# Gated delta layer, sample tokens: four heads stacked on 128 rows instead of one head at a time

## The reference, cut to what matters

```python
gc = jnp.cumsum(gc, axis=-1)
a_mat = bc[..., :, None] * einsum('nbhid,nbhjd->nbhij', kc, kc) * decay_strict + eye(L)
rhs = concatenate([bc[..., None] * vc, (bc * exp(gc))[..., None] * kc], axis=-1)
sol = triangular_solve(a_mat, rhs, lower=True, unit_diagonal=True)
aqk = einsum('nbhid,nbhjd->nbhij', qc, kc) * decay_incl
def step(S, c):
    u = wv_c - einsum('bhlk,bhkv->bhlv', wk_c, S)
    o = einsum('bhlk,bhkv->bhlv', qg_c, S) + einsum('bhij,bhjv->bhiv', aqk_c, u)
    S = gl_c[..., None, None] * S + einsum('bhlk,bhlv->bhkv', kd_c, u)
    return S, o
```

## Time and profile before

| what | value |
|---|---|
| median of 3 runs | 3318.43 us |
| lowest, highest | 3312.52, 3320.44 us |
| the profiled execution | 3321.11 us, its span 3319.2 us |
| mean granted clock of PE over the span | 0.942 of 2.4 GHz |
| gated delta stage, output of the projection to the next stage | about 1811 to 2244 us of the span |
| data moved | HBM read 385.00 MB, written 14.57 MB |

### The profile page before, as it was taken

The page is one execution under the profiler, slowest core; times in us unless marked ns, Lnnn a source line. Parts: engine busy times, 40 slices in busy tenths (PEclk is TensorE's granted clock), DMA queues, the critical chain, the costliest instruction groups (busy, mean ns, idle before and its releaser), DMA issues.

```text
span 3319.2 us, 62869 instructions
## 1 busy us (share of the span) xinstructions
PE 3116.9 (94%) x28140; PEld 2778.6 (84%) x28140; DVE 1560.3 (47%) x2515; ACT 1076.9 (32%) x1630; POOL 146.8 (4%) x261
## 2 busy tenths in 40 slices
PE   7998998999999899999999998689999989998998
PEld 6995788799999665999998677359999957787997
DVE  4644543465564124464653534235556544534554
ACT  3432222344443122343432322013444332222342
POOL 1000001100000110000000100100000000011000
PEclk9999998899999896999998999569999999998999
DMA  7452401353635451445444230215454424111541
GB/s 221 146 164 80 141 4 32 102 169 130 195 129 200 154 193 52 135 145 186 155 130 153 102 106 8 63 51 175 131 188 146 145 72 153 52 29 44 164 138 67
DMA packets 333440, 402.41 MB, mean 121 GB/s; under 512 B 14746, under 2 KB 287295, under 8 KB 332813
## 3 DMA queue, kind: packets, MB, share of 16 engines
q1 hardware_dynamic: 320176, 353.20, 32.8%
q0 software_dynamic: 13072, 46.41, 4.8%
HBM read 385.00 MB, written 14.57 MB: 120 GB/s over the span
## 4 chain that ended last, share of the span: by engine, by line
PE 91%; DVE 5%; ACT 2%; issue 1%; POOL 0%; DMA 0%; DVEq 0%; ACTq 0%; POOLq 0%
PE bank L804 17%; PE bank L806 17%; PE bank L805 17%; PE bank L837 11%; PE bank L1417 4%; PE bank L1108 2%; PE bank L913 2%; PE bank L799 2%; PE bank L873 1%; PE bank L889 1%; PE bank L1652 1%; PE bank L1087 1%; PE bank L1639 1%; PE bank L1061 1%; PE bank L1192 1%
## 5 line engine op out<-in xcount | busy, mean ns | idle before, releaser
L804 PE MATMUL bank<-h_hi,w_hi 128*128 128x288 f32 x2816 | 837.0, 297 | 5.5 <-DVE h_lo L2119 5.5
L805 PE MATMUL bank<-h_hi,w_lo 128*128 128x288 f32 x2816 | 831.3, 295 | 0.0
L806 PE MATMUL bank<-h_lo,w_hi 128*128 128x288 f32 x2816 | 828.5, 294 | 0.0
L2127 DVE TENSOR_TENSOR w_lo<-ring,w_hi 128x2048 fp32r<-128x2048 f32 (+1 forms) x304 | 611.1, 2011 | 413.6 <-ACT w_hi L1736 413.6
L1736 ACT CAST w_hi<-ring 128x2048 fp32r<-128x2048 f32 (+1 forms) x304 | 511.1, 1683 | 613.1 <-PE bank L806 568.6
L804 PEld LDWEIGHTS bank<-h_hi,w_hi 128*128 128x128 f32 x2816 | 528.2, 188 | 6.7 <-DVE w_lo L2127 6.0
L806 PEld LDWEIGHTS bank<-h_lo,w_hi 128*128 128x128 f32 x2816 | 530.8, 188 | 0.0
L805 PEld LDWEIGHTS bank<-h_hi,w_lo 128*128 128x128 f32 x2816 | 529.1, 188 | 0.6
L804 PE MATMUL bank<-hid_hi,w_hi 128*128 128x288 f32 x1408 | 416.1, 296 | 0.0
L805 PE MATMUL bank<-hid_hi,w_lo 128*128 128x288 f32 x1408 | 415.4, 295 | 0.0
L806 PE MATMUL bank<-hid_lo,w_hi 128*128 128x288 f32 x1408 | 414.3, 294 | 0.0
(11 more groups left out here) (516 smaller groups left out, 3550.5 us busy)
## 6 DMA issues: line engine op xcount, KB each, us to landing
ring<-in_ffn_w_gate SPq DMA_DIRECT2D x88, 1024.0 KB, 5.5
ring<-in_ffn_w_up SPq DMA_DIRECT2D x88, 1024.0 KB, 8.0
ring<-in_ffn_w_down SPq DMA_DIRECT2D x64, 768.0 KB, 4.7
ring<-in_ffn_w_down SPq DMA_DIRECT2D x64, 640.0 KB, 5.9
ring<-in_rwkv_w_rkv SPq DMA_DIRECT2D x24, 1024.0 KB, 7.3
ring<-in_gdn_w_in SPq DMA_DIRECT2D x16, 1024.0 KB, 7.2
ring<-in_attn_w_qkv SPq DMA_DIRECT2D x12, 1024.0 KB, 6.4
ring<-in_rwkv_w_o SPq DMA_DIRECT2D x8, 1024.0 KB, 6.5
```

Source lines behind the costliest of these rows:

```text
L804: nc.tensor.matmul(out, w_hi_k, x_hi_k, start=start, stop=False)
L805: nc.tensor.matmul(out, w_lo_k, x_hi_k, start=False, stop=False)
L806: return nc.tensor.matmul(out, w_hi_k, x_lo_k, start=False, stop=stop)
L2127: nc.vector.tensor_tensor(w_lo[e][:, 0:k, :], raw, w_hi[e][:, 0:k, :], ALU.subtract).then_inc(w_lo_ready, 1)
```

## The change

The sample tokens of four heads are stacked on 128 partitions: head 4a + q has its 32 tokens on partitions 32q to 32q + 31 (ROWS), so there are two stacks (a = 0, 1) instead of eight heads of 32 partitions. The gates of the samples are projected into that layout, with four columns a product instead of 16.

Token-major copies, Gram matrices and decays of all eight heads come right after the start of the first ladder, and their two-level inverse between its levels. All eight states of a stack are held at a time (S0[0], S0[1], 2 MB each): the first four heads are loaded where the first two were, the other four after chunk 2's read, into memory of the first ladder. State reads stand between the pieces of chunks 2 and 3. The reads of four heads share one bank, are copied once, turned once, and solved with a product for each head. Decays of the sample states go from DVE to POOL; keys masked by sequence are made by POOL (sKmask) instead of masked u by DVE. The updates are four rounds, each of two halves (four sequences) of one stack: 16 products of 32 x 128 weights with 128 columns that take turns over the four row groups and write four banks, and four DVE additions of 128 x 512. Rounds 0 and 1 stand before the head norms, round 2 inside them, round 3 inside the projection. The norms and the projection use banks 4 to 7 first, and PE waits for the fifth addition to x before the next stage. POOL's mask and decay products come after the convolution instead of in it. Stores of the first four heads are issued after round 1, of the others after round 3.

```diff
-                for k in range(CH):
-                    last = nc.tensor.matmul(bank[4][0:NS, 64:80], h[:, k, SEQ:], w[:, k, :], start=(k == 0), stop=(k == CH - 1))
+                    for q, r in enumerate(ROWS):
+                        last = nc.tensor.matmul(bank[4][r, 64:68], h[:, k, SEQ:], w[:, k, :].rearrange(...)[:, q], ...)
...
+                gdn_read(2)
+                gdn_turn(1)
+                sample_read(0)
+                gdn_solve(2)
+                sample_read(1)
+                gdn_query(2)
+                gdn_update(2)
+                sample_read(2)
+                sample_read(3)
+                gdn_read(3)
+                gdn_turn(2)
+                sample_turn_read(0)
+                gdn_solve(3)
+                gdn_query(3)
+                sample_read(4)
+                gdn_update(3)
+                for hd in (5, 6, 7):
+                    sample_read(hd)
                 gdn_turn(3)
+                sample_turn_read(1)
+                for a in range(2):
+                    gdn_sample_solve(a)
                 after(goT_ready)
+                for a in range(2):
+                    gdn_sample_output(a)
+                after(seq_rows_ready, 2)
                 after(gs_ready)
+                sample_update(0)
+                after(got_ready, 2)
+                for a in range(2):
+                    last = nc.tensor.transpose(bank[3][:, 128 * a:128 * a + 128], sO[:, a, :], ident)
+                last.then_inc(goT_raw, 1)
+                after(goT_ready)
+                sample_update(1)
+                pe.wait_ge(gs_ready, NCHUNK + 1)
+                head_norms(0, 4, GDN_NORM_BANK, lambda: sample_update(2))
+                after(og_ready, 4)
...            (round 3 before block 2 of the projection; before block 4 a wait for its additions)
+                square(b + 9, W(GO_), 4, last_updates)
+                pe.wait_ge(x_updated, 8 * (s + 1) + 5)
...
+            def sample_matrices_gdn():
+                for i, src in enumerate((2, 1)):
+                    for a in range(2):
+                        for q, r in enumerate(ROWS):
+                            last = nc.tensor.matmul(bank[4 + i][r, 128 * a:128 * a + 128], W(src)[:, q + 4 * a, SEQ:], ident, ...)
+                for a in range(2):
+                    for q, r in enumerate(ROWS):
+                        last = nc.tensor.matmul(bank[6][r, 64 * a:64 * a + 64], W(1)[:, q + 4 * a, SEQ:], work[:, 0:2, q + 4 * a, SEQ:], ...)
+                after(g_spread)
+                for a in range(2):
+                    for r in ROWS:
+                        last = nc.tensor.matmul(bank[7][r, 32 * a:32 * a + 32], sG[r, a, :], const("causal4")[r, 0:32], ...)
+            def sample_inverse_start():      # 16 products, after level 2; sample_inverse_y and _x: 8 each, level 3
+            def sample_read(hd):
+                a, q = divmod(hd, 4)
+                if q == 0:
+                    after(gstate_in[a], 64)
+                for b_ in range(DEC_B):
+                    c0 = SEQ + DEC_T * b_
+                    last = nc.tensor.matmul(out[:, :, q, b_, :], S0[a][:, q, b_, :], work[:, 0:2, hd, c0:c0 + DEC_T], ...)
+            def gdn_sample_solve(a):
+                after(sr_ready)
+                for r in ROWS:
+                    last = nc.tensor.matmul(bank[a][r, 0:128], sXT[r, a, :], sR[r, a, :], start=True, stop=True)
+            def sample_update(i):            # PE
+                a, bh = divmod(i, 2)
+                if i >= 2:
+                    pe.wait_ge(gs_ready, NCHUNK + i)
+                for j in range(4):
+                    for q, r in enumerate(ROWS):
+                        last = nc.tensor.matmul(bank[ROUND_BANK[i][q]][:, 128 * j:128 * j + 128], sKmask[r, 4 * bh + j, a, :], sU[r, a, :], ...)
...
+                def sample_update(i):        # DVE
+                    after(gs_raw)
+                    after(gs_decayed)
+                    for q in range(4):
+                        part_ = S0[a][:, q, 4 * bh:4 * bh + 4, :].rearrange("p b n -> p (b n)")
+                        last = TT(part_, part_, bank[ROUND_BANK[i][q]][:, :], ALU.add)
...
+                def decayed_states(a):       # POOL
+                    for bh in range(2):
+                        part_ = S0[a][:, :, 4 * bh:4 * bh + 4, :]
+                        nc.gpsimd.tensor_tensor(part_, part_, egLs[...].broadcast_to([128, 4, 4, 128]), ALU.mult)
...
+                for a in range(2):           # POOL
+                    pool.wait_ge(gs_ready, NCHUNK + 2 + 2 * a)
+                    for q in range(4):
+                        pool.dma_start(dst[4 * a + q], S0[a][:, q]).then_inc(gstate_stored[a], 16)
```

More of the change, by code:

```diff
@@ L657, in program @@
+        sQK, sN, sY, sXT = (hflat[:, 2048 + 64 * i:2112 + 64 * i].rearrange("p (a n) -> p a n", n=32) for i in range(4))
+        sRead = cut(8192, (2, 2, 128))
+        sO = cut(8704, (2, 128))
+        sKmask = work[:, 2, :, 0:256].rearrange("p b (a n) -> p b a n", a=2)
+        ROUND_BANK = ((4, 5, 6, 7), (0, 1, 2, 3), (0, 1, 2, 3), (0, 1, 2, 3))
+        GDN_NORM_BANK = (5, 6, 7, 4, 5, 6, 7, 4)
         conv_in = shift_in
@@ new lines, in sample_inverse_start @@
+            def sample_inverse_start():
+                after(gtok_ready)
+                after(inv_start)
+                for a in range(2):
+                    for w in range(2):
+                        for r in ROWS:
+                            xt, one = sY[r, a, :], const("ident32")[r]
+                            last = nc.tensor.matmul(bank[4][r, 64 * a + 32 * w:64 * a + 32 * w + 32], one if w else xt, xt if w else one,
+                                                    start=(a == 0 and w == 0), stop=False, skip_group_check=True)
+                last.then_inc(inv_raw, 1)
@@ new lines, in sample_inverse_y, with sample_inverse_x @@
+            def sample_inverse_y():
+                after(inv_ready)
+                for a in range(2):
+                    for r in ROWS:
+                        last = nc.tensor.matmul(bank[5][r, 32 * a:32 * a + 32], sN[r, a, :], sX[r, a, 0, :], start=True, stop=True)
+                last.then_inc(invy_raw, 1)
+            def sample_inverse_x():
+                after(invy_ready)
+                for a in range(2):
+                    for r in ROWS:
+                        last = nc.tensor.matmul(bank[4][r, 64 * a + 32:64 * a + 64], sY[r, a, :], sX[r, a, 1, :],
+                                                start=False, stop=True, skip_group_check=True)
+                last.then_inc(inv_raw, 1)
@@ L1555, in gdn_inverse @@
                     gdn_query(0)
+                else:
+                    sample_matrices_gdn()
                 for l in range(1, LADDER):
@@ L1573, in gdn_inverse @@
                             gdn_turn(0)
+                    else:
+                        if l == 3:
+                            sample_inverse_y()
+                        if l == 4:
+                            after(inv_ready)
                     for g in range(2):
@@ L1583, in gdn_inverse @@
                         last.then_inc(inv_raw, 1)
+                    if not p and l == 2:
+                        sample_inverse_start()
+                    if not p and l == 3:
+                        sample_inverse_x()
                 if p:
@@ L2648, in gdn @@
-                dve.wait_ge(goT_ready, 4 + GH)
+                read(2)
+                solve(2)
+                update(2)
+                read(3)
+                solve(3)
+                sample_rhs(0)
+                update(3)
+                sample_rhs(1)
+                for a in range(2):
+                    after(su_raw)
+                    V.tensor_scalar(sU[:, a, :], bank[a][:, 0:128], gcol[:, BETA, 2, a:a + 1], None, ALU.mult).then_inc(su_ready, 1)
+                for a in range(2):
+                    last = V.tensor_scalar(sO[:, a, :], bank[2 + a][:, 0:128], gcol[:, EGC, 2, a:a + 1], None, ALU.mult)
@@ L2649, in gdn @@
+                link(last)
+                for a in range(2):
+                    after(go2_raw)
+                    TT(sO[:, a, :], sO[:, a, :], bank[a][:, 128:256], ALU.add).then_inc(got_ready, 1)
+                for i in range(2):
+                    sample_update(i)
+                dve.wait_ge(goT_ready, NCHUNK + 1)
                 for c in range(CH):
```

454 lines of the change are left out of this document (177 added, 277 removed).

## The result

The changed kernel took 3213.56 us (median of four runs, 3207.45 to 3219.08), the one before 3317.75 (3312.52 to 3320.44): a ratio of 0.9687, 95% interval 0.9664 to 0.9711. The forecast was 3217, range 3202 to 3240. The profiled execution took 3219.08 us, span 3216.4, against 3321.11 and 3319.2, so 102 us less where the working had 101.

The account below looks back on a forecast made before the run. Bound: a serial chain per head, ending on PE each time. B to F sum to 100.5 us against 205.4; with A, -101 from 3321.1 gives 3220, and 3217 as the runs' median (range 3202 to 3240).

Parts of the forecast that it names:

- the likeliest case: Whole kernel: the stage's chain shortened, the clock falling in some reads and recovering; 3217 us, chance 0.46.
- A: Sample work moved into the earlier prompt ladder, where PE is the bound, adds +4 us (3 to 7).
- B: Chunk 2's read to the sample solve: two chunk turns and eight state reads take about 39 us.
- C: Sample solve and first update round, until head sums may start: 7.5 us (5.7 to 10).
- D: Head norms, with round 2 in the reciprocal's wait: 16 us (12.1 to 18.1).
- E: Output projection plus round 3 on PE: 35.4 us (32.2 to 37.5).
- F: Stage's end: late state stores hold up weight casts and additions to x, +2.6 us (1 to 8).
- Rival 1: The clock stays at 2.4 GHz through the stage: a gain of 122.5 us, 3196 us; chance 0.14.
- rival 2: The clock is low from the first read to the projection: a gain of 84 us, 3234 us; chance 0.20.
- Rival 3: Groups don't overlap in the inserted products and update rounds: +16 us, 3233 us; chance 0.09.
- Rival 4: The second four states' stores land 13 us later, during the projection: 3230 us; chance 0.08.

Follow-up runs that it names:

- e6: Kernel after with all eight sample state reads in one block behind chunk 3's update: 3220.43 us, ratio 0.9715.
- e8: Kernel after with only one of the eight products of each state read: 3188.61 us.
- e2: Kernel after with each row group's four update products issued one after another instead of in turn: 3214.97 us.
- e3_double: Kernel after with the samples' token-major and Gram products issued twice in the ladder: 3205.92 us.
- e10: Kernel before with the next head's read issued behind the output product, its copy later, and a third state buffer: 3291.6 us, ratio 0.9923.
- e13_decays_late: Kernel after with GpSimd's decay of the first four states waiting for the last chunk: 3208.35 us, ratio 0.968.
- e11_wide_fill: Kernel after with wider reads, three unused products in the reciprocal's wait, and the reciprocal behind five of eight DVE products: 3200.38 us, ratio 0.9652.
- e4_no_store: Kernel after with the stores of the second four sample states left out: 3209.34 us.
- e1_wide: Kernel after with each state read product taking its own and all later sequences' columns, 64 down to 8: 3211.35 us, ratio 0.9686.
- e5_fill: Kernel after with five unused 288-column products in PE's wait for the norms' reciprocal: 3206.57 us, ratio 0.9676.
- e12_after_again: Kernel after, unchanged, run again as the measure for the others: 3213.9 us, ratio 0.9684.

## Why the prediction was right, point by point

The mechanism was that of the likeliest case: one chain in place of eight, PE without idle time through reads and projection, the clock in between. The sizes, forecast against the two profiles of the kernel after (first, again):

| term | forecast | first | again |
|---|---|---|---|
| A, into the ladder | +4 | +0.9 | +2.5 |
| B, reads and chunks | 39 | 37.3 | 33.1 |
| C, solve and round | 7.5 | 5.8 | 6.8 |
| D, norms | 16 | 14.5 | 16.3 |
| E, projection | 35.4 | 35.3 | 34.9 |
| F, late at the end | +2.6 | +1.2 | +1.1 |
| rest of the program | 0 | +7.2 | +8.1 |

*A* was too large. The 128 inserted records are there at the size forecast (3.4 us, each group counted to the start of the next product; 3.3 forecast), but the four column groups of the gate projection took no time on top of what was there (64 records in 1.04 us, as 16 did before), and the ladder has one low stretch of 3.4 us fewer in the first profile. With two of them in both kernels the difference is 2.5.

*B* was right in its mean (clock 0.70 and 0.80 around a forecast of 0.75): full clock first, a fall in the first reads, recovery, a fall in the last. But the clock fell four times in the first profile and not twice. Two readings of the working were off as well: its rows add up to 5.97 us of PE a chunk and not 5.7, and the earlier trace rows leave 3.4 us of idle for both chunks together and not 2.3 for each. The forecast's reason for the order, that the reads fill the gaps of the chunks, counts for little: e6 has the chunks alone at 13.6 us with 1.8 idle. The reads are added time, and their price is doubled by the clock that they bring down (e8). Rival 1 (no fall) and rival 2 (a fall throughout) are both refuted by the windows; e8 shows rival 1's clock when the reads are taken out, e6 most of rival 2's when they are not interrupted.

*C*: the terms that the working names (2.15 for the small steps, 1.7, 2.8) add up to 6.65, and it takes 7.5 without saying why. A round takes 1.17 us, not 1.7, and the four additions 2.5, not 2.8. The Trainium skill (TensorE: Matmul & The Clock Gate, Part 3), from which the prediction worked out an estimate of about 35 ns a record beside its own term, was the nearer of the two. Rival 3 (the groups do not overlap) is the kernel e2: its rounds cost 4.0 us more each at the low clock, as that rival had it, but 1.7 more at the full one, and the stage 7.7 and not 16. What decides between the two is the order of the issue.

*D and E* were right within 1.5 us. *F* had the right chain and nearly its times: the stores landed 25.4 us into the projection (forecast 26), the first addition to x began at 32.0 (32.4). The additions then came every 0.80 us, not every 0.97, so the norm was held up 1.1 to 1.2 us and not 2.6. Rival 4 (stores 13 us late) did not occur.

What failed is a sentence that the prediction did not write: that the rest of the program keeps its time. Ladder and stage together came out 9.6 us better than forecast (174.4 against 164.8, the norm's start included) and the rest 7.2 us worse, so that the total met this closely is luck: two errors of opposite sign. Thirteen profiles of this study have the same instructions behind the stage, and their time there goes with how long the clock is low in it:

| profile | clock low in the rest, us | rest, us |
|---|---|---|
| e3_double | 56.2 | 1064.5 |
| e10 (kernel before, early read) | 62.9 | 1067.8 |
| e13_decays_late | 65.5 | 1071.5 |
| before | 69.4 | 1071.8 |
| e8_few_reads | 72.6 | 1069.0 |
| e2_no_turns | 72.9 | 1072.0 |
| e11_wide_fill | 73.0 | 1073.3 |
| e6_reads_late | 79.8 | 1075.4 |
| e4_no_store | 85.5 | 1076.2 |
| e1_wide | 86.5 | 1076.0 |
| e5_fill | 86.6 | 1075.9 |
| after | 92.5 | 1079.0 |
| e12_after_again | 97.1 | 1079.9 |

From the first row to the last it is 15.4 us for 40.9, so 0.38 us for each microsecond of low clock. That the clock differs there though the code is the same is measured; that it depends on the moment at which the program arrives there fits, but no run set that moment by itself, and it stays open. The part ahead of the ladder speaks against the edits as the only cause: it begins with the program and no experiment touches it, and it took from 1962.6 us (e13, 129.7 of them at the low clock) to 1972.8 (e3, 160.4). So at least some of this comes with the single execution. It also bounds what the whole can tell: an edit that costs 5 us in the stage (e13, e2) can vanish in it.

## What to carry to other kernels

When a serial chain of small steps repeats per head, stack the heads on the unused partitions, and issue products of different row groups in turn: the overlap tried alone gave a quarter of the gain here. Price dense products of few columns at the low clock, and alternate them with others (1 to 5 us here) or give them more columns, which cost a read nothing here (1.85 us at full clock either way). Keep GpSimd's long two-input instructions away from VectorE's on SBUF. Judge edits of a few microseconds by their own stretch and several profiles, not by the whole.

## What the runs showed of the hardware

- A DVE product with two SBUF inputs took 5.89 us instead of 0.44 beside two GpSimd products of 3.6 us each; it began during the first and got through only behind both. DVE additions from PSUM beside the same work took their usual 0.62.
- A read of sixteen records of 128x128 weights takes 1.85 us at 2.4 GHz with 8 moving columns a record and with 64 down to 8.
- The granted clock fell to half in stretches in which PE was busy all the time: 18 of 23 us of uninterrupted reads of 8 columns (e6).
- Four row groups in turn: 34 to 37 ns a record of 128 columns at full clock; the same products group by group 88 ns.
- Five unused products in a 2.6 us wait shortened the low stretch behind it from 13.7 to 6.8 us and the spreads' sixteen records from 8.01 to 5.11 (e5 beside e4); three, with the reciprocal sooner, the spreads from 8.01 to 4.56 (e11 beside e1).
